# Encoder layer on one Trainium2 core: the first weight piece's high part made on VectorE, two token tiles weighted and scaled on GpSimd

## What is computed

```python
def rms_norm(x, w):
    xf = x.astype(jnp.float32)
    y = xf * lax.rsqrt(jnp.mean(xf * xf, axis=-1, keepdims=True) + NORM_EPS)
    return (y * w.astype(jnp.float32)).astype(x.dtype)
...
    xn = rms_norm(x, norm1_w)
    proj = xn @ w_in
    hq, hf_f, hf_b, hi, hg, aq, ak, av = jnp.split(proj, split_points(), axis=-1)
    o_hg = hgrn2_bidirectional(hq, hf_f, hf_b, hi, hg, lb_f, lb_b, hg_norm_w)
    o_da = diff_attention(aq, ak, av, layer, q_norm_w, k_norm_w, lq1, lk1, lq2, lk2, subln_w)
    h = x + (jnp.concatenate([o_hg, o_da], axis=-1) @ w_out).astype(x.dtype)
    return h + expert_choice_moe(rms_norm(h, norm2_w), router_w, w1, w3, w2)
```

## Time and profile before

| | |
|---|---|
| median of three runs | 2013.2 us (2013.1 to 2015.03) |
| profiled execution, time | 2015.22 us |
| profiled execution, span | 2013.4 us |
| PE busy | 1982.5 us, 98% |
| DVE busy | 1621.6 us, 81% |
| ACT busy | 1303.9 us, 65% |
| POOL busy | 78.9 us, 4% |

### The profile page before, as it was taken

How to read it: one execution, slowest core, us unless ns; L and a number is a source line. 1 busy time by engine, 2 the same in 40 slices (tenths; PEclk the granted TensorE clock), 3 DMA queues, 4 the chain that set the end, 5 groups by cost and what they waited for, 6 DMA issues and landing times.

```text
span 2013.4 us, 26132 instructions
## 1 busy us (share of the span) xinstructions
PE 1982.5 (98%) x9770; PEld 1656.2 (82%) x9770; DVE 1621.6 (81%) x1247; ACT 1303.9 (65%) x1000; POOL 78.9 (4%) x50
## 2 busy tenths in 40 slices
PE   9999999999899999999999999999999999999998
PEld 8888888778688888888888888888888888888886
DVE  5258877865788888888888988888888889888886
ACT  5234434743677777777777777777777777777774
POOL 0000000100000000000000000000000000000000
PEclk9999999999899999999999999999999999999999
DMA  5212314235799999999999999999999999999994
GB/s 162 64 53 84 114 65 147 84 125 201 270 390 362 406 367 389 379 383 389 377 394 364 400 363 404 366 387 380 382 384 383 385 371 398 362 406 364 395 379 160
DMA packets 217984, 615.98 MB, mean 306 GB/s; under 512 B 14833, under 2 KB 57073, under 8 KB 217938
## 3 DMA queue, kind: packets, MB, share of 16 engines
q1 hardware_dynamic: 214096, 602.70, 79.7%
q0 software_dynamic: 3696, 12.59, 2.7%
q10 hardware_dynamic: 146, 0.07, 0.0%
HBM read 595.66 MB, written 19.66 MB: 306 GB/s over the span
## 4 chain that ended last, share of the span: by engine, by line
PE 94%; DVE 4%; ACT 1%; issue 1%; DMA 0%; POOL 0%; ACTq 0%; POOLq 0%
PE pair L727 29%; PE pair L729 29%; PE pair L728 29%; PE pair L847 2%; PE pair L1206 1%; PE pair L950 1%; PE pair L1144 1%; PE pair L917 0%; DVE neg_max L1851 0%; PE pair L1039 0%; PE pair L897 0%; DMA raw_w<-w_in 0%; PE pair L937 0%; PE pair L762 0%; DVE wo_low L1905 0%
## 5 line engine op out<-in xcount | busy, mean ns | idle before, releaser
L2185 DVE TENSOR_TENSOR chunk_low<-ring,chunk_high 128x3072 fp32r<-128x3072 f32 (+1 forms) x384 | 1180.5, 3089 | 197.4 <-ACT chunk_high L1542 195.6
L1542 ACT ACTIVATE chunk_high<-ring 128x3072 fp32r<-128x3072 f32 (+1 forms) x384 | 983.5, 2570 | 329.3 <-PE pair L729 329.3
L727 PE MATMUL pair<-chunk_high,xe_high 128*128 128x512 f32 x1408 | 551.2, 391 | 1.0 <-DVE xe_low L2179 1.0
L729 PE MATMUL pair<-chunk_high,xe_low 128*128 128x512 f32 x1408 | 548.4, 390 | 0.0
L728 PE MATMUL pair<-chunk_low,xe_high 128*128 128x512 f32 x1408 | 547.7, 389 | 0.0
L729 PEld LDWEIGHTS pair<-chunk_high,xe_low 128*128 128x128 f32 x1408 | 264.2, 188 | 55.7
L727 PEld LDWEIGHTS pair<-chunk_high,xe_high 128*128 128x128 f32 x1408 | 264.3, 188 | 54.9 <-ACTq L1588 1.2
L728 PEld LDWEIGHTS pair<-chunk_low,xe_high 128*128 128x128 f32 x1408 | 264.4, 188 | 54.1
L727 PE MATMUL pair<-chunk_high,hid_high 128*128 128x512 f32 x704 | 276.9, 393 | 0.0
L729 PE MATMUL pair<-chunk_high,hid_low 128*128 128x512 f32 x704 | 274.5, 390 | 0.0
L728 PE MATMUL pair<-chunk_low,hid_high 128*128 128x512 f32 x704 | 274.0, 389 | 0.0
(11 more groups left out here) (265 smaller groups left out, 1778.0 us busy)
## 6 DMA issues: line engine op xcount, KB each, us to landing
ring<-w SPq DMA_DIRECT2D x240, 1536.0 KB, 9.0
ring<-w SPq DMA_DIRECT2D x128, 1024.0 KB, 8.8
ring<-w SPq DMA_DIRECT2D x32, 768.0 KB, 8.7
raw_w<-w_in SPq DMA_DIRECT2D x40, 256.0 KB, 2.9
ring<-w SPq DMA_DIRECT2D x32, 256.0 KB, 6.5
ring<-w SPq DMA_DIRECT2D x16, 512.0 KB, 10.0
raw_w<-w_in SPq DMA_DIRECT2D x6, 1024.0 KB, 5.6
wo_raw<-w_out SPq DMA_DIRECT2D x8, 512.0 KB, 3.3
```

The source lines that it names most:

```text
L727: pe.matmul(dst, a_high, b_high, start=first, stop=False)
L729: return pe.matmul(dst, a_low, b_high, start=False, stop=last)
L1542: act.activation(ch[c % SPLIT][:, 0:n], ring[c % RING][:, 0:n], ACT.Copy).then_inc(ch_done, 1)
L2185: dve.tensor_tensor(cl[c % SPLIT][:, 0:n], ring[c % RING][:, 0:n], ch[c % SPLIT][:, 0:n].bitcast(F32), ALU.subtract).then_inc(cl_done, 1)
```

## The change

ACT's `high_part(0)` goes; DVE makes that part itself (`first_high_part`), in the place where `scale(2)` and `scale(3)` stood. Those two tiles go to GpSimd, each in two operations: the product with the norm's weight (`weighted`), which needs the tile and `norm1_bc` alone, and the multiplication by the reciprocal root (`scale`), which needs `mean_and_rstd(1)`. As GpSimd writes the product into `x_scaled` while ACT may still square the same tile, the squares' unneeded output goes to another buffer (`qk_raw`, not in use yet). The semaphore `masks_done` is replaced by one more count of `setup_v`.

```diff
+        squares_of = [qk_all[:, 2 * i:2 * i + 2, :, :].rearrange("p q t n -> p (q t n)")[:, 0:D] for i in range(2)]
+
         def squares(i):
             t = ORDER[i]
             act.wait_ge(x_tile_in[t], 16)
-            act.activation(x_scaled[:, t, :], x_in[:, t, :], ACT.Square, accum_out=stat1[:, i:i + 1]).then_inc(x_sq, 1)
+            if i >= 2:
+                act.wait_ge(x_sq, i - 1)
+            act.activation(squares_of[i % 2], x_in[:, t, :], ACT.Square, accum_out=stat1[:, i:i + 1]).then_inc(x_sq, 1)
...
         x_high(0)
         x_high(1)
-        high_part(0)
         x_high(2)
...
+        def first_high_part():
+
+            dve.wait_ge(w_in_sem[0], 16)
+            dve.tensor_copy(wh[0][:, :, :], raw_w[:, :, :]).then_inc(wh_done, 1)
+
...
         scale(0)
         scale(1)
         mean_and_rstd(1)
-        scale(2)
-        scale(3)
+        first_high_part()
         x_low(0)
         x_low(1)
         low_part(0)
...
-        dve.tensor_copy(masks[:, :, :], masks_f[:, :, :]).then_inc(masks_done, 1)
-        dve.wait_ge(masks_done, 1)
+        dve.tensor_copy(masks[:, :, :], masks_f[:, :, :]).then_inc(setup_v, 1)
+        dve.wait_ge(setup_v, 13)
...
+        def scale(i):
+            t = ORDER[i]
+            pool.wait_ge(x_rstd, i // 2 + 1)
+            pool.wait_ge(x_normed, i - 1)
+            pool.tensor_scalar(x_scaled[:, t, :], x_scaled[:, t, :], rstd1[:, i:i + 1], None, ALU.mult).then_inc(xs_ready, 1)
+
+        def weighted(i):
+            t = ORDER[i]
+            pool.wait_ge(x_tile_in[t], 16)
+            pool.tensor_tensor(x_scaled[:, t, :], x_in[:, t, :], norm1_bc[:, :], ALU.mult).then_inc(x_normed, 1)
+
+        pool.wait_ge(norm1_done, 2)
+        weighted(2)
+        weighted(3)
+        scale(2)
+        scale(3)
         for a in range(ATT_UNITS + 4):
```

More of the change, by code:

```diff
@@ L321, in build @@
     head_norms_in = sem("head_norms_in")
-    masks_done = sem("masks_done")
     norm2_in = sem("norm2_in")
@@ L333, in build @@
     x_sq = sem("x_sq")
+    x_normed = sem("x_times_norm_weight")
     x_std = sem("x_std")
```

## The result

The changed kernel takes 2021.11 us (median of 7 runs, 2020.88 to 2023.88), the kernel before, on the same chip, 2014.18 (median of 7). The ratio is 1.0036 with a 95% interval of 1.0027 to 1.0045: slower by 0.36%, or 7 us. The range on record ended at 2017.6, so the time lies outside it, on the side of the fourth rival but not by its cause. The forecast stood on a median of 2013.2 for the kernel before; 1.0 us of the miss of 5.4 is that base, the rest is the change, 6.9 us where 2.5 was forecast.

The account below looks back on a forecast made before the run. PE, 98% busy, was taken as the bound, so only the start of its unbroken work counts. VectorE's path +2.2 and PE's +1.6 to +3.9 were taken as +2.5 over 2013.2: 2015.7 us, range 2012.9 to 2017.6.

Parts of the forecast that it names:

- the fourth rival: PE's second fill and third transpose stay at 1.2 GHz after holes in its early work; time 2018.1, chance 0.14.
- The start of PE's unbroken work decides, and what is behind it only moves along: First plain-loop matmul (L727), at 30.42 before: early changes matter only by moving it, and the span moves with it.
- The cast on VectorE, 1.22: VectorE's new high part of the first weight piece, 2048 elements, takes 1.22 us; upper bound 2.29.
- Its wait for the landing: VectorE's cast needs the weight piece landed at 11.5; in the worked sum it starts only at 13.95.
- GpSimd's product, 2.1: Each GpSimd product of a tile with the norm weight, 1024 elements, takes about 2.1 us.
- Mutual waits between the products and `scale`, +2.1 at the first `x_low`: GpSimd's products and VectorE's `scale` exclude each other in turn; first `x_low` begins at 15.17 instead of 13.03.
- The one-input multiplication, 1.3 with bounds of 1.0 and 2.1: GpSimd's multiplication by the reciprocal root takes 1.3 us, between the memset's 1.0 and the product's 2.1.
- scale(3) till 17.6: GpSimd's second multiplication ends at 17.6, with VectorE's `w_low` following just as GpSimd lets go, ending at 19.8.
- PE's path: Third transpose at 16.8 instead of 14.39, then 15.2 us of work: +1.6, or up to +3.9 at a low clock.
- the case that the prediction worked out: Start of the plain loop with mutual waits in turn: VectorE's path +2.2; likeliest time 2015.7, chance 0.52.

Follow-up runs that it names:

- the kernel without multiplications: Changed kernel with GpSimd's two multiplications by the reciprocal root left out, tiles 2 and 3 staying unscaled by it: 2017.30 us, 1.0014 of the kernel before.
- the changed kernel's second profile: The changed kernel with nothing altered, measured once more beside the kernel before: 2024.33 us against 2013.72, ratio 1.0044.
- more fill: Changed kernel with 10 more fill calls (20 matmuls) on PE ahead of the fourth transpose, run twice: 2021.69 and 2020.94 us.
- the constant factor: Changed kernel with GpSimd's multiplications by the constant 1.0 instead of the per-token value: 2022.59 us, 1.0043 of the kernel before.
- the run of lengths: Kernel before, with probe operations (products, multiplications, copies) on idle GpSimd over unused buffers between 26 and 95 us: 2014.72 us, ratio 1.0003.

## Why the prediction was wrong

- **The start of PE's unbroken work decides, and what is behind it only moves along: right.** The start moved by 7.5, the span by 7.3.
- **The cast on VectorE, 1.22: right**, 1.23. Its wait for the landing was covered, as forecast.
- **GpSimd's product, 2.1: nearly.** 2.35 without a meeting (in the kernel without multiplications the first one). The rows that it was taken from are squares, which read one buffer twice; so did the probe's product, with 2.03 and 1.89. The Trainium skill's GPSIMD Engine Reference, section Performance versus the Vector engine, has 4497 ns for an addition of two fp32 tensors of 2048 elements; half of it, as an estimate, is 2.25, close to the 2.35.
- **Mutual waits between the products and `scale`, +2.1 at the first `x_low`: right in kind, a little small.** It came to 2.8 (`x_low` from 15.83 instead of 13.03). In the profiled execution tile 2 landed only at 7.75, so the second `scale` was held and not the first, and then the mean (2.33 for 0.16) by the second product: a place at which no wait was forecast. In the changed kernel's second profile the product began at 7.25 and the order was the forecast one, both `scale` held (2.97 and 3.37), the mean not (0.15). The sum was much the same, with `x_low` from 15.66.
- **The one-input multiplication, 1.3 with bounds of 1.0 and 2.1: the step that failed.** It takes 2.85, outside both bounds. The argument was that it reads one operand where the product reads two. The copy, which also reads one, does take 1.04; the multiplication doesn't follow the number of operands. Two of them are 5.7 instead of 2.6.
- **"scale(3) till 17.6": failed by its size first, and then by the order that followed.** Being that long, the second multiplication met `w_low`. The prediction had, for a length of 2.1, `w_low` wait for GpSimd. It went the other way: `w_low` began at 18.10, half a microsecond before the first multiplication ended and not held by it, and GpSimd waited from 18.63 to about 20.2. Tile 3 came at 23.1.
- **PE's path: the wrong transpose was watched.** The third was traced (16.8 forecast, 18.69 measured). The fourth, which stands in PE's list ahead of all further products, waits for `scale(3)`; it was assumed to follow in time, and with 17.6 it would have. At 23.14 instead of 16.25 it carries 6.9 us, less 0.8 of room, plus the 1.6 that the clock takes behind the hole.
- **The clock (fourth rival): half right.** Its slow fill is real: 3.51 in the kernel without multiplications, where the third transpose started at 19.01 (19.2 forecast for a low clock) and the plain loop 3.6 later than before (3.9 forecast). In the changed kernel it costs little, since GpSimd has tile 2 ready only at 18.6: the third transpose starts at 18.69 behind a fill of 2.17, and at 18.99 behind one of 4.05 (more fill, which is the same kernel up to there). The fall that counted came later, behind the hole in front of the fourth transpose, and cost 1.6 in the traces, shown by the added fill.

Put together at the start: the kernel without the multiplications is 3.6 over before, which is the case that the prediction worked out (2.2 for VectorE's path, up to 3.9 for PE's at the low clock); the multiplications add the other 3.9, 2.3 by the later tile 3 and 1.6 by the clock behind it. With the multiplications short, on ScalarE, the shift is 3.2 us, inside the 4.4 that the range allowed over its base. With 2.85 in place of 1.3, `scale(2)` would have ended at 17.85 and `scale(3)`, behind `w_low`, near 22.5 by the prediction's own steps, and that alone gives +5.4 at the start (16.25 to 22.5, less 0.8).

## What to carry to other kernels

An operation whose length no row shows is not bounded by rows of other operations because it "reads less"; when the whole sum hangs on it, its upper bound must be left open, and the range with it. Follow each moved result to every instruction that stands behind its reader in an in-order list, not only the first one: the wait that counted was at the second reader. And two moves that each cost little (1 us and 3 us) can meet on a shared access and cost 7 together: apart, GpSimd's tile 3 was ready at 20.24, just under PE's own 20.76; together, the waits for the cast and for `w_low` brought it out to 23.1.

## What was not expected of the hardware

**How long GpSimd shuts VectorE out.** A product does so nearly for its whole length: the `scale` of 3.39 above takes 1.28 alone, so it was let in at 10.69, 0.2 us before the product's end at 10.89. (All such times suppose that an operation runs at its own pace once it is let in.) The multiplication does so for about its first microsecond only. In the run of lengths, VectorE in order of time:

```profile
29.54 0.86 DVE L1654 TENSOR_TENSOR lambda_products<-lambda_rows 128x64 f32<-128x64 f32 x1
...
32.34 0.90 DVE L1673 TENSOR_SCALAR one_minus_lb<-lb 128x8 f32<-128x8 f32 x1
...
38.44 2.95 DVE L1601 TENSOR_TENSOR w_low<-raw_w,w_high 128x2048 fp32r<-128x2048 f32 x1 [0.78 <-ACT w_high L1226]
```

GpSimd's multiplications began at 29.20, 32.15 and 38.13. The `w_low` takes 2.29 alone, so it was let in at 39.10, 0.97 after GpSimd's start, and the last 1.9 us of the multiplication ran beside it. `one_minus_lb`, 0.17 alone, was let in at 33.07, 0.92 after the start. That fits the `w_low` at 18.86 above, 1.45 after its multiplication's start, which was not held at all. The Trainium skill, SBUF — State Buffer, section Who interferes with whom, has the loser blocked for the whole instruction; for the product this case's traces agree, for the multiplication they don't (0.97 of 2.85). Why the hold ends so early was not tried and stays open.

**Small operations are held as well**: the mean of 128 x 2 elements took 2.33 under a product, 0.16 without.

**The clock's course differs between executions of one kernel.** The fill of 18 took 2.17 in one profiled execution of the changed kernel and 2.71 in the other; with more fill, a kernel that is the same up to that point, it took 4.05 and 3.76. Nor does the fall follow the length of the hole alone: in the changed kernel's first profile the work behind the hole of 3.56 ran at 1.00, while with the constant factor it ran at 0.50 behind a hole of 1.94. How much of the scatter of 1 to 2 us between executions comes from this is not shown.
